# Two-layer hybrid decoder trunk: Toeplitz column products moved ahead of the states, a block copied by group, down tiles over eight PSUM banks, and finer hand-overs between queues

## What is computed

```
for l in range(2):
    h = rms_norm(x, norm1_g[l]) * (1 + sc1) + sh1
    u, cq, ckv, kr, gate_a, gate_b = split(h @ w_in[l])
    y_a = s5_mixer(u, ...) @ w_a_out[l]        # 32 groups of 16 channels, 64 complex states each
    y_b = mla_mixer(cq, ckv, kr, ...) @ w_b_out[l]     # 8 heads, low-rank queries and keys
    x = x + g1 * ((sigmoid(gate_a) * y_a + sigmoid(gate_b) * y_b) @ w_out[l])
    h = rms_norm(x, norm2_g[l]) * (1 + sc2) + sh2
    x = x + g2 * ((silu(h @ w_gate[l]) * (h @ w_up[l])) @ w_down[l])   # inner width 2816
return rms_norm(x, final_g)
```

## Time and profile before

| what | before |
|---|---|
| median of three runs | 3152.47 us |
| the profiled execution | 3150.09 us |
| its span, first to last instruction | 3147.9 us |
| mean granted PE clock | 0.987 |
| busy: PE, PEld, DVE, ACT, POOL | 3044.4, 2559.9, 1546.8, 986.5, 870.6 us |
| instructions | 36605 |

### The profile page before, as it was taken

One profiled execution on the slowest core, in us unless ns is written; L12 is line 12 of the kernel. 1 busy time (PEld: TensorE's weight loads), 2 busy tenths in 40 slices (PEclk: granted clock), 3 DMA queues, 4 the chain that ended last, 5 costly groups with the idle time before them and its releaser, 6 DMA issues.

```text
span 3147.9 us, 36605 instructions
## 1 busy us (share of the span) xinstructions
PE 3044.4 (97%) x14672; PEld 2559.9 (81%) x14672; DVE 1546.8 (49%) x1949; ACT 986.5 (31%) x1397; POOL 870.6 (28%) x512
## 2 busy tenths in 40 slices
PE   6999999999999999999999999999999999999998
PEld 5787889978878888888878888898787888888886
DVE  7865487855133232232379885786524222232224
ACT  3422367751231111111142225777223111111112
POOL 0334222222422222222244542222232222222223
PEclk9999999999999999999999999999999999999999
DMA  7555400124221222111125651002331111111111
GB/s 269 170 157 156 154 13 12 51 61 155 79 75 61 62 78 63 61 61 47 47 101 168 187 175 55 14 25 51 121 135 40 51 50 47 47 47 47 48 53 67
DMA packets 278932, 264.25 MB, mean 84 GB/s; under 512 B 46706, under 2 KB 237298, under 8 KB 277619
## 3 DMA queue, kind: packets, MB, share of 16 engines
q1 hardware_dynamic: 252464, 217.66, 22.7%
q10 hardware_dynamic: 26306, 44.32, 3.8%
HBM read 218.59 MB, written 40.96 MB: 82 GB/s over the span
## 4 chain that ended last, share of the span: by engine, by line
PE 80%; DVE 7%; issue 5%; ACT 4%; DMA 2%; POOL 1%; SPq 1%; ACTq 1%; DVEq 0%; POOLq 0%
PE ps L550 22%; PE ps L552 22%; PE ps L553 21%; PE ps L1321 3%; PE ps L1307 2%; PE ps L1341 2%; PE ps L1342 2%; PE ps L1302 2%; PE ps L1306 2%; DVE x_sb L2420 1%; DVE silu L2402 1%; DMA raw<-in_w_in 1%; ACT hid_hi L1536 1%; PE ps L1186 1%; PE ps L1168 1%
## 5 line engine op out<-in xcount | busy, mean ns | idle before, releaser
L534 POOL TENSOR_TENSOR wlo<-raw,whi 128x1024 fp32r<-128x1024 f32 (+3 forms) x288 | 543.4, 1895 | 1963.6 <-ACT whi L526 1963.6
L526 ACT ACTIVATE whi<-raw 128x1024 fp32r<-128x1024 f32 (+3 forms) x290 | 242.8, 859 | 1637.5 <-PE ps L553 1480.5
L550 PE MATMUL ps<-h_hi,whi 128*128 128x512 f32 x2176 | 701.0, 396 | 25.8 <-DVE h_lo L2042 18.2
L552 PE MATMUL ps<-h_lo,whi 128*128 128x512 f32 x2176 | 692.3, 392 | 0.0
L553 PE MATMUL ps<-h_hi,wlo 128*128 128x512 f32 x2176 | 691.7, 392 | 0.0
L550 PEld LDWEIGHTS ps<-h_hi,whi 128*128 128x128 f32 x2176 | 409.3, 190 | 114.3 <-DVE h_lo L2042 22.2
L552 PEld LDWEIGHTS ps<-h_lo,whi 128*128 128x128 f32 x2176 | 412.8, 190 | 86.7
L553 PEld LDWEIGHTS ps<-h_hi,wlo 128*128 128x128 f32 x2176 | 411.8, 189 | 87.4
L2402 DVE TENSOR_TENSOR silu<-silu,ps 128x1024 f32<-128x1024 f32 x44 | 53.7, 1221 | 769.4 <-PE ps L553 760.2
L2420 DVE SCALAR_TENSOR_TENSOR x_sb<-ps,mod,x_sb 128x1024 f32<-128x1024 f32 x160 | 203.2, 1280 | 178.0 <-PE ps L553 178.0
L550 PE MATMUL ps<-hid_hi,whi 128*128 128x512 f32 x704 | 224.8, 393 | 9.5 <-DVE x_sb L2420 9.5
(11 more groups left out here) (250 smaller groups left out, 4250.9 us busy)
## 6 DMA issues: line engine op xcount, KB each, us to landing
ada_raw<-in_w_ada SPq DMA_DIRECT2D x64, 512.0 KB, 4.5
raw<-in_w_in SPq DMA_DIRECT2D x92, 256.0 KB, 4.7
raw<-in_w_gate SPq DMA_DIRECT2D x88, 256.0 KB, 3.2
raw<-in_w_up SPq DMA_DIRECT2D x88, 256.0 KB, 3.3
raw<-in_w_down SPq DMA_DIRECT2D x88, 256.0 KB, 2.8
gate_scratch<-gst ACTq DMA_DIRECT2D x32, 512.0 KB, 3.8
gl<-gate_scratch SPq DMA_DIRECT2D x32, 512.0 KB, 4.1
ada_rows<-in_w_ada SPq DMA_DIRECT2D x16, 512.0 KB, 5.6
```

Of the source, the lines that this page charges most:

```text
L526: last = act.activation(dst(whi[:, s, :]), src(raw[:, s, :]), ACT.Copy)
L534: last = pool.tensor_tensor(dst(wlo[:, s, :]), src(raw[:, s, :]), dst(whi[:, s, :].bitcast(F32)), ALU.subtract)
L550: pe.matmul(o, w_h, x_h, start=first, stop=False)
L552: pe.matmul(o, w_h, x_l, start=False, stop=False)
```

## The change

In the order of the diff:

- Down tiles use banks 2(t % 4) and the next, so all eight; tiles 0 to 3 wait for the multiplication of gate and up that frees their banks, tiles 4 to 7 for the addition of the tile four before. The waits of the next chunk's gate and up products and of the last chunk follow.
- `toe_g` holds the Toeplitz block with the groups outermost. ACT copies `toe` into it by one instruction in part 2 (`batch_by_group`), and PE waits for that (`toe_ready`) and no longer for the DMAs.
- The column products move on PE from `batch_states` to the end of `batch_transposes`; on DVE the addition into `toe_col` moves to the head of `states`, before the wait for the products with the states.
- SP brings `ut` of batches 1 to 7 one t later in the first layer; in the second layer nothing moves.
- ACT splits the first gate unit before the exponential and the sine of the mixer's parameters, and takes the sine after the first two copies of u.
- The gelu of the last batch's outputs moves behind the norm of the latents, its four DMAs behind `latent_hi`.
- The sides of the first head pair in attention come one step later.
- The first merge tile waits for each `yg_lo` by itself. The residual comes back in two DMAs.
- The low parts of three weight units move from POOL to DVE (`weight_lo`): the second and third of each feed-forward block and the second of the second layer.
- In the final norm PE adds the last square by accumulation, and POOL's last addition goes.

```diff
+        toe_g = sb("toe_g", [P, 4, CH, M])
+        toe_ready = count("toe_ready", 8)
-        x_back = count("x_back", 16)
+        x_back = [count("x_back_first", 16), count("x_back_rest", 16)]
@@ side_of
-                    return ((VS, 0, 1), (KO, 0, 0), (KO, 0, 1), None, None, None)[g]
+                    return (None, (VS, 0, 1), (KO, 0, 0), (KO, 0, 1), None, None)[g]
@@ sync
-                    if t >= 3 and t % 2 and (t - 3) // 2 < 8:
-                        ut_load((t - 3) // 2)
+                    b, odd = divmod(t - 1 - S5_LAG[l] // 2, 2)
+                    if t == 3:
+                        ut_load(0)
+                    elif 0 < b < 8 and not odd:
+                        ut_load(b)
@@ tensor, batch_transposes
                     last.then_inc(s5_tr.sem, 1)
+                    wait(pe, toe_col_done, l, b)
+                    for g in range(4):
+                        last = pe.matmul(ps[:, 6, g * M:(g + 1) * M], be[:, b % 2, g, :, :].rearrange("p j m -> p (j m)"),
+                                         c_n[:, first_group(b) + g, :], start=True, stop=True)
+                    last.then_inc(toe_col_mm.sem, 1)
@@ batch_outputs
-                    wait(pe, toe_loaded, l, 16 * CH * (b + 1))
+                    wait(pe, toe_ready, l, b + 1)
-                        pe.matmul(o, toe[:, j, :, :, g].rearrange("p r m -> p (r m)"), ut[:, j, g, :], start=True, stop=False)
+                        pe.matmul(o, toe_g[:, g, :, :].rearrange("p r m -> p (r m)"), ut[:, j, g, :], start=True, stop=False)
@@ merge
-                        wait(pe, yg_ready, l, 4)
-                    end = tile_products(pe, j, 4 * j, yg_hi, yg_lo, [(k, k) for k in range(4)])
+                    for k in range(4):
+                        if t == 0:
+                            wait(pe, yg_ready, l, k + 1)
+                        end = tile_products(pe, j, 4 * j, yg_hi, yg_lo, [(k, k)], first=(k == 0), last=(k == 3))
@@ down_products
-                            b = 2 * (t % 2)
-                            if t < 2:
-
-                                pe.wait_ge(up_done.sem, up_done.at(l, 2 * c_static + (2 if last_chunk else 3)) + c_reg * 2)
-                                pe.wait_ge(dn_ev.sem, dn_ev.at(l, 8 * (c_static - 1) + 7 + t) + c_reg * 8)
+                            b = 2 * (t % 4)
+                            if t < 4:
+
+                                pe.wait_ge(up_done.sem, up_done.at(l, 2 * c_static + 3 + t // 2) + c_reg * 2)
                             else:
-                                pe.wait_ge(dn_ev.sem, dn_ev.at(l, 8 * c_static + t - 1) + c_reg * 8)
+                                pe.wait_ge(dn_ev.sem, dn_ev.at(l, 8 * c_static + t - 3) + c_reg * 8)
@@ scalar
+                split_hi(act, l, U_GATE)
                 wait(act, s5_dve, l, S5_EXP_READY)
                 act.activation(sm[:, S_MAG:S_MAG + 2, :], sm[:, S_AD:S_AD + 2, :], ACT.Exp).then_inc(s5_act.sem, 1)
-                wait(act, s5_dve, l, S5_ANGLES_READY)
-                act.activation(trig[:, :, :], sm[:, 0:6, :], ACT.Sin).then_inc(s5_act.sem, 1)
-                split_hi(act, l, U_GATE)
                 wait(act, x_spilled, l, 16)
                 for n, (ct, side) in enumerate(U_ORDER):
+                    if n == 2:
+                        wait(act, s5_dve, l, S5_ANGLES_READY)
+                        act.activation(trig[:, :, :], sm[:, 0:6, :], ACT.Sin).then_inc(s5_act.sem, 1)
...
+                def batch_by_group(b):
+                    wait(act, toe_loaded, l, 16 * CH * (b + 1))
+                    copy(toe_g[:, :, :, :], toe[:, b % 2, :, :, :].rearrange("p r m g -> p g r m")).then_inc(toe_ready.sem, 1)
+
...
-                s5_part(4 * KT + 5)
                 latent_scale(0)
                 latent_rms(1)
+                s5_part(4 * KT + 5)
@@ vector
+            def weight_lo(l, n):
+
+                s = n % 2
+                wait(dve, w_hi_done, l, n + 1)
+                wait(dve, w_lo_done, l, n)
+                apart(dve)
+                lo_of(wlo[:, s, :], raw[:, s, :], whi[:, s, :]).then_inc(w_lo_done.sem, 1)
+
...
                 def states(b):
+                    wait(dve, toe_col_mm, l, b + 1)
+                    wait(dve, toe_loaded, l, 16 * CH * b)
+                    dve.tensor_tensor(toe_col[:, :, :].rearrange("p m g -> p g m"), d_col[:, first_group(b):first_group(b) + 4, :],
+                                      ps[:, 6, 0:4 * M].rearrange("p (g m) -> p g m", g=4), ALU.add)\
+                        .then_inc(toe_col_done.sem, 1)
                     wait(dve, v_mm, l, b + 1)
...
-                for k in range(1, 6):
+                hidden_lo(l, 2, 1)
+                weight_lo(l, U_FFN + 1)
+                for k in range(2, 6):
                     hidden_lo(l, 2, k)
...
-                        dve.scalar_tensor_tensor(x_sb[:, t, :], pair(2 * (t % 2)), mod[:, 5, t:t + 1], x_sb[:, t, :],
+                        dve.scalar_tensor_tensor(x_sb[:, t, :], pair(2 * (t % 4)), mod[:, 5, t:t + 1], x_sb[:, t, :],
```

More of the change, by code:

```diff
@@ L1054, in _ @@
                 add_squares(l, 1, 1, KT - 2)
-                split_lo(pool, l, U_FFN + 1)
                 add_squares(l, 1, 1, KT - 1)
+                wait(pool, w_lo_done, l, U_FFN + 3)
                 apart(pool)
@@ L1059, in _ @@
                     for j in range(6):
-                        split_lo(pool, l, U_FFN + 2 + j, 3 * i)
-                for n in range(UNITS - 4, UNITS):
+                        split_lo(pool, l, U_FFN + 3 + j, 3 * i)
+                for n in range(UNITS - 3, UNITS):
                     split_lo(pool, l, n)
@@ L1065, in _ @@
                     add_squares(l + 1, 0, 0, k)
-                for k in range(1, KT):
+                for k in range(1, KT if l + 1 < DEPTH else KT - 1):
                     if k == 4 and l + 1 < DEPTH:
@@ L1169, in batch_states @@
                     last.then_inc(v_mm.sem, 1)
[L1170 to L1174, removed]
                 def batch_outputs(b):
@@ L1517, in _ @@
                             unit_ready(pe, l, UNITS - 2 + d)
[L1519 removed]
+                        wait(pe, dn_ev, l, 8 * last_chunk + (n - 3 if n >= 4 else n // 2 - 3))
                         for k in range(2):
@@ L1528, in _ @@
                             norm_scale(l + 1, 0)
-            mean_squares(DEPTH, 1)
+            wait(pe, sq_added[1], DEPTH, KT - 2)
+            for part in range(2):
+                if part:
+                    wait(pe, sq_ready[1], DEPTH, KT)
+                for t in range(4, TT):
+                    rows = (sq_sum[:, t * P:(t + 1) * P], sq_ring[:, 2 + (KT - 1) % 2, (t - 4) * P:(t - 3) * P])[part]
+                    last = pe.matmul(ps[:, 6, t:t + 1], rows, mean_col[:, :], start=(part == 0 and t == 4),
+                                     stop=(part == 1), skip_group_check=True)
+            last.then_inc(sq_mm.sem, 1)
             norm_scale(DEPTH, 1)
@@ L1656, in s5_part @@
                             batch_toeplitz(b)
+                        elif part == 2:
+                            batch_by_group(b)
                         elif part == 3:
@@ L1837, in _ @@
                 wait(act, x_spilled, l, 16)
-                act.dma_start(x_sb[:, :, :], xs_dram).then_inc(x_back.sem, 16)
+                for part, tiles in enumerate((slice(0, 2), slice(2, KT))):
+                    act.dma_start(x_sb[:, tiles, :], xs_dram[:, tiles, :]).then_inc(x_back[part].sem, 16)
                 for n in range(KT - 2):
@@ L1842, in _ @@
                     wait(act, wo_ev, l, n + 1)
+                    if n == 0:
+                        for part in x_back:
+                            wait(act, part, l, 16)
                     for t in range(2):
@@ L2363, in _ @@
                               mg_hi[:, tile, :].rearrange("p o n -> p (o n)")).then_inc(mg_ready.sem, 1)
-                wait(dve, x_back, l, 16)
-                apart(dve)
                 for n in range(KT - 2):
+                    if n in (0, 2):
+                        wait(dve, x_back[n // 2], l, 16)
+                        apart(dve)
                     wait(dve, unit_used, l, U_OUT + n + 1)
```

22 lines of the change are left out of this document (10 added, 12 removed).

## The result

| | before | after |
|---|---|---|
| median | 3152.64 us (3152.0 to 3154.65) | 3119.14 us (3115.66 to 3120.97) |
| ratio, 95% interval | | 0.9891 [0.9874, 0.9908] |
| the profiled execution, its span | 3150.09, 3147.9 us | 3115.66, 3113.6 us |
| mean granted PE clock | 0.987 | 0.99 |

The change makes the kernel 33.5 us faster, where 69.5 were forecast, and 3119 lies above the range of 3060 to 3110. The profiled execution of after is the fastest of its four, so its sums run to 34.4 us.

The account below looks back on a forecast made before the run. PE, busy for 97% of the span, was taken as the bound. Ten gains summed to 69.5 us, taking the profiled 3150.09 to 3080.6; 2.4 added for the median gave 3083.0, range 3060 to 3110.

Parts of the forecast that it names:

- First-layer gates: First layer's batches: moving `ut` nearly ends PE's wait for `mt`; 29.93 to 26.9 us a batch, gain 21.2, ends 0 and 29.
- Rival A: First-layer gates: the wait only moves and a batch stays at 29.9 us; total 3104.2 us; chance 20%.
- Rival C: 16-byte step not the cause of slow loads, and the chunk's wait reappears at gate and up products; 3111.9 us; 6%.
- Rivals B and D: B: more gained than forecast, 3064.8 us, 12%. D: slower, clock falling in the eight-bank down stage, up to 3519, 4%.
- Down tiles: Feed-forward chunks: eight banks remove the wait for the addition to `x_sb`; 0.8 us in 20 chunks, gain 16.0.
- The copy by group: Outputs of the other nine batches: `toe_g` makes weight loads cheaper; gain 6.2 us, ends 0 and 8.6.
- Merge: First merge tile: taking `yg_lo` one by one covers the wait and spares half-clock stretches; gain 10.1 us, lower end 4.
- feed-forward start: Start of each feed-forward block: low parts on DVE shorten PE's waits; gain 4.0 us over two layers.
- first gate unit: ACT splits it before the sine, so PE's 3.38 us wait for `wlo` shrinks; gain 4.7 us, ends 0 and 5.0.
- Layer boundary: Second layer's start: the second unit's low part goes to DVE; estimated gain 0.7 us, ends 0 and 1.7.
- Attention start: First head pair's sides one step later, so `v_st` is ready; gain 2.0 us a layer, 4.0 in all.
- Latents: Last gelu and its DMAs leave the head of ACT's queue; gain 1.5 us, ends 0 and 2.5.

Follow-up runs that it names:

- (1): The changed kernel with the modulation rows loaded one t later in the first layer: 3086.33 us, ratio 0.9775.
- (9): The changed kernel with first-layer modulation rows one t later, plus the second layer's sine before the split of the first gate unit, as before the change: 3078.79 us, 0.9773.
- (11): The changed kernel with first-layer modulation rows one t later, plus the first head pair's sides one step earlier, as before the change: 3083.38 us, 0.9792.
- (4): The changed kernel without the copy by group, outputs reading `toe` and waiting for the DMAs: 3128.15 us, ratio 0.991.

## Why the prediction was wrong

- **First-layer gates: the failed step.** "The queue that it leaves delivers the even unit 2.48 us sooner, so `mt` is about that much sooner, and the wait of 2.52 is nearly gone." The first half is wrong in size: counted from the end of `h_st`, `mt` came 1.7 us sooner, with the weights now close behind 1 MB of rows, and the product gained only 1.1, since it then waited for the late `ut`. The forecast had no wait for `ut` at all. The second is wrong in kind. The wait isn't an amount of lateness that can be paid off; it is the difference between the loop and PE's 26 us, and the loop closes through DVE and the modulation rows. With the loop cut (1) the period is 26.1, and 26.9 had been taken. The end "0" of the term was too high as well: the stretch lost 7.8 us, 4.4 of them, as I read it, by the head start that is waited off, and the rest by the three edits, with the longer DVE half among them.
- **What the forecast saw and priced wrongly.** "The queue that it is moved into now has the 2.48 us ahead of the odd unit." That was right. As I read the rows, it put the odd unit's `wlo` on POOL beside DVE's operations, where 1.9 us a batch are lost.
- **Rival A** named the mechanism's outcome, a wait that only moves and a batch that stays at 29.9, and would have given 3104.2. It had 20% and was the nearest in kind; the first layer's gates and latents came out 9.4 us longer than by it (7.8 lost, 1.6 gained in its sum), and the boundary and attention some 5 us. **Rival C**, at 3111.9, has the nearest number by luck, for the wrong reasons: the stride was the cause, the chunk's wait did not reappear. **Rivals B and D** did not come. D in a row of after, with the down tiles over eight banks and the clock at 1.00:

```profile
960.00:1550.00 590.00, 590.00 (x2605) 488.54 (x2604) 177.99 (x140) 93.81 (x91) 131.65 (x55) 1.00 0.20 61
```

PE idles nowhere in it. The Trainium skill, page "TensorE: Matmul & The Clock Gate", section "A second HAM failure mode: psum-queue depth-cycling", tells of a clock that swings in a kernel that cycles through banks with short idle times between its groups of products; in this stretch there are no idle times and no swing.
- **Down tiles: right.** The first down product of two chunks nine apart starts at

```profile
958.38 0.61 PE L552 MATMUL ps<-hid_hi,whi 128*128 128x512 f32 x2
```

```profile
1545.90 0.61 PE L552 MATMUL ps<-hid_hi,whi 128*128 128x512 f32 x2
```

(1545.90 - 958.38)/9 = 65.28 us, 0.79 less than the 66.07 of the earlier trace rows, times 20 = 15.7. The choice near the load's wait and not PE's own was right.
- **The copy by group: right in the second layer.** Loads 199 ns, batches 25.9, and PE idles once for the outputs, for 0.42 us. The copy took 1.13 us, where 0.96 was estimated. In the first layer PE idles 1.0 to 1.9 us for it in five batches, which it has to spare while the loop is longer: without the copy it idles as well (4).
- **Merge, feed-forward start, end, first gate unit: right**, each within 1.1 us.
- **Layer boundary: wrong sign.** The second unit's low part on DVE does take away a wait of 1.4 us; the step that failed is "Late next is the second unit or u's own copies". It looked at the first layer alone. In the second the late sine held up DVE's tables and with them `be`, for 3.0 us (9).
- **Attention start:** the stall went to what the forecast should have named: `probs`, the next thing that PE needs there (11). The 1.6 us lost in the steps behind it aren't shown to be the change's: those steps take 263.2, 264.8 or 266.5 us a layer in the kernels tried here, with either place of the sides.
- **Latents:** their 1.5 us can't be told apart from the gates here.

A chance of 58% on a forecast with 21 of 69.5 us on one loop was too much, and the range should have reached down to where that term is negative.

## What to carry to other kernels

Where a wait comes back at the same distance in every pass of a loop, follow the chain round until it meets itself; only a link of the circle, or cutting it, changes the period, and a head start in front of it is waited off. A releaser in a timeline can be the wrong one of several: compare its end with the start that it is said to have allowed. If two stages run the same work and one is slower, compare where their queues stand against each other first: here the second layer's order, carried over to the first in one line, gave 33 us, as much as the whole change. When an instruction is moved past a transfer, ask not only who waits for it but what now runs beside whom.

Kernel 9 beats both, at 3078.79 us, 0.9773 of before.

## What the hardware showed that was not expected

- A DVE operation of 128 x 512 with all operands in SBUF took 0.69 us while POOL was idle, 1.58 beside POOL's operations of the same size, and 2.47 beside POOL's subtraction of 128 x 1024; the four scans behind it took 1.37, 3.17 and 3.98. The three before it, with one input in PSUM, took 0.69 each, also beside the subtraction. The Trainium skill, page "SBUF — State Buffer", section "Who interferes with whom", says that a DVE instruction with two SBUF inputs contends with a GpSimd instruction that reads SBUF, and that one with at most one SBUF input, outside the two-port modes, doesn't. The rows agree.
- ACT's copy of 128 x 512 with a step of 16 bytes took 1.13 us, 1.9 times the 0.60 of a contiguous one; PE's load of weights at the same step 1.6 times, 319 ns against 199. By the same page's "Door 1: The DMA port swizzle" each new 16-byte line costs; the size is the trace's.
- In the batch shown, the last transfer of the even unit's weights landed 4.33 us after its issue in before, and 5.86 in the changed kernel, where SP turned to these weights 1.5 us after it began to issue two rows of 512 KB, in place of 4.2.
